# The end of the last output product: token tile by token tile, with four stores of 256 KB

## The reference

```
def rms_norm_2(x, g):
    xf = x.astype(jnp.float32)
    y = xf * lax.rsqrt(jnp.mean(xf * xf, axis=-1, keepdims=True) + RMS_EPS)
    return (y * g.astype(jnp.float32)).astype(x.dtype)

def swiglu_ffn(x, w_in, w_out):
    gate, up = jnp.split(x @ w_in, 2, axis=-1)
    return (jax.nn.silu(gate) * up) @ w_out

# second_block, for each of two layers; h after the last one is the result, 256 x 1024
        normed = rms_norm_2(h, ffn_norm_pre[layer])
        h = h + rms_norm_2(swiglu_ffn(normed, ffn_w_in[layer], ffn_w_out[layer]), ffn_norm_post[layer])
```

## Time and profile before

| | us |
|---|---|
| median of 3 runs | 1220.99 (1220.68 to 1221.53) |
| the profiled execution | 1221.12 |
| its span | 1219.1 |
| PE busy in the span | 1185.5 (97%) |
| DVE, ACT, POOL busy | 758.5, 600.0, 151.6 |

### The profile page before, as it was taken

One profiled execution on the slowest core, in us unless ns is written; L12 is line 12 of the kernel. 1 busy time (PEld: TensorE's weight loads), 2 busy tenths in 40 slices (PEclk: granted clock), 3 DMA queues, 4 the chain that ended last, 5 costly groups with the idle time before them and its releaser, 6 DMA issues.

```text
span 1219.1 us, 19296 instructions
## 1 busy us (share of the span) xinstructions
PE 1185.5 (97%) x7504; PEld 1052.2 (86%) x7504; DVE 758.5 (62%) x1049; ACT 600.0 (49%) x862; POOL 151.6 (12%) x175
## 2 busy tenths in 40 slices
PE   6999999998999999999999999999799989999997
PEld 6999999997888887888888888888799968888885
DVE  5667544376887555564535777764676866777752
ACT  6665553434544444543434544443566756445431
POOL 2000000051123001211100111100101101111100
PEclk9999999999999999999999999999899999999999
DMA  9455344543555654645435455465444234554540
GB/s 355 176 208 190 105 139 173 176 168 139 178 202 177 245 184 160 227 160 186 173 133 212 156 176 195 180 220 194 146 153 160 70 109 173 211 198 172 179 166 34
DMA packets 31975, 212.06 MB, mean 174 GB/s; under 512 B 4169, under 2 KB 4829, under 8 KB 7592
## 3 DMA queue, kind: packets, MB, share of 16 engines
q1 hardware_dynamic: 28936, 201.68, 46.6%
q0 software_dynamic: 2688, 9.26, 2.2%
q10 hardware_dynamic: 288, 0.23, 0.1%
HBM read 210.08 MB, written 1.08 MB: 173 GB/s over the span
## 4 chain that ended last, share of the span: by engine, by line
PE 86%; issue 6%; DVE 3%; ACT 2%; POOL 2%; DMA 1%; SPq 0%; DVEq 0%; POOLq 0%; ACTq 0%
PE acc L446 41%; PE acc L585 17%; PE acc L587 8%; PE aux L446 8%; PE acc L486 1%; POOL gate L795 1%; PE acc L488 1%; PE acc L490 1%; PE acc L539 1%; PE acc L536 1%; PE acc L541 1%; PE aux L2579 1%; PE aux L2640 1%; PE aux L2228 1%; ACT wh L419 1%
## 5 line engine op out<-in xcount | busy, mean ns | idle before, releaser
L427 DVE TENSOR_TENSOR wl<-raw,wh 128x2048 fp32r<-128x2048 f32 x129 | 295.2, 2294 | 259.7 <-ACT wh L419 253.0
L419 ACT ACTIVATE wh<-raw 128x2048 fp32r<-128x2048 f32 x190 | 362.7, 1912 | 144.9 <-PE acc L446 109.9
L585 PE MATMUL acc<-hx,wh 128*128 128x512 f32 x864 | 305.4, 399 | 0.0
L587 PE MATMUL acc<-hx,wl 128*128 128x256 f32 x864 | 242.7, 281 | 0.0
L446 PE MATMUL acc<-hx,wh 128*128 128x256 f32 x1280 | 234.6, 285 | 1.9 <-DVE hx L662 1.9
L446 PEld LDWEIGHTS acc<-hx,wh 128*128 128x128 f32 x1280 | 200.7, 193 | 3.4 <-DVE wl L427 2.1
L585 PEld LDWEIGHTS acc<-hx,wh 128*128 128x128 f32 x864 | 162.4, 188 | 40.4
L446 PE MATMUL acc<-hx,wl 128*128 128x256 f32 x640 | 181.7, 284 | 0.0
L587 PEld LDWEIGHTS acc<-hx,wl 128*128 128x128 f32 x864 | 163.2, 189 | 0.0
L434 DVE TENSOR_TENSOR wl<-raw,wh 128x1024 fp32r<-128x1024 f32 x122 | 151.9, 1245 | 1.5 <-ACT wh L419 1.0
L446 PEld LDWEIGHTS acc<-hx,wl 128*128 128x128 f32 x640 | 123.3, 193 | 0.0
(11 more groups left out here) (382 smaller groups left out, 1948.2 us busy)
## 6 DMA issues: line engine op xcount, KB each, us to landing
raw<-in_stream SPq DMA_DIRECT2D x190, 1024.0 KB, 4.8
bias_b<-in_bias POOLq DMA_DIRECT2D x6, 512.0 KB, 4.6
grow<-in_grows POOLq DMA_DIRECT2D x4, 512.0 KB, 4.3
nbias<-strip POOLq DMA_DIRECT2D x4, 512.0 KB, 4.6
x<-in_x SPq DMA_DIRECT2D x2, 512.0 KB, 4.0
y<-x SPq DMA_DIRECT2D x1, 1024.0 KB, 3.9
s<-cums POOLq DMA_DIRECT2D x1, 512.0 KB, 4.2
decay<-in_decay POOLq DMA_DIRECT2D x1, 512.0 KB, 3.8
```

Source lines behind the costliest of these rows:

```text
L419: nc.scalar.activation(wh[:, s, :], raw[:, s, :], ACT.Copy).then_inc(hi_ready, 1)
L427: nc.vector.tensor_tensor(wl[:, s, :], raw[:, s, :], wh[:, s, :].bitcast(F32), ALU.subtract).then_inc(lo_ready, 1)
L585: nc.tensor.matmul(out[:, :], wh[:, s, cols], hx[:, k].rearrange("p a n -> p (a n)"), start=(k == 0), stop=False, skip_group_check=True)
L587: last = nc.tensor.matmul(out[:, 0:SEQ], wl[:, s, cols], hh[:, k, :], start=False, stop=(k == KT - 1), skip_group_check=True)
```

## The change

PE runs the last two chunks of the last layer's output product token tile by token tile: tile 0 of o0+9 and of o0+10, then tile 1 of both. The other layer's product keeps its order. The last norm uses the form by token tile on ACT, DVE and POOL. SP issues four stores of 128 rows by 512 columns (256 KB), in the order tile 0 left, tile 0 right, tile 1 left, tile 1 right, each behind the semaphore of the instruction that writes that part of `x`, and waits for all four.

```diff
-            sp.wait_ge(post_done, 4 * TT)
-            sp.dma_start(io["out"].rearrange("(t p) d -> p t d", p=P), x[:]).then_inc(y_out, 16)
-            sp.wait_ge(y_out, 16)
+            for t in range(TT):
+                for half in range(2):
+                    cols = slice(half * WW, (half + 1) * WW)
+                    sp.wait_ge(*((post_done, 3 * TT + t + 1) if half else (x_half, 2 * TT + t + 1)))
+                    sp.dma_start(io["out"][t * P:(t + 1) * P, cols], x[:, t, cols]).then_inc(y_out, 16)
+            sp.wait_ge(y_out, 16 * 2 * TT)
@@ pool
-            post(3)
+            for t in range(TT):
+                pool.wait_ge(mean_in, 2 * TT + t + 1)
+                g.tensor_tensor(rstd[:, t:t + 1], psum1[:, t:t + 1], mhalf[:, 0:1], ALU.pow).then_inc(mean_pow, 1)
@@ scalar
-            post(3, "ffn_out_1", (6, 5), fjunk, 1)
+            o0 = START["ffn_out_1"]
+            for c in range(o0 + 4, o0 + 9):
+                split_hi(act, c)
+            for t in range(TT):
+                tile_square(3, "ffn_out_1", 0, t, fjunk)
+            for c in range(o0 + 9, o0 + 11):
+                split_hi(act, c)
+            for t in range(TT):
+                tile_square(3, "ffn_out_1", 1, t, fjunk)
@@ vector
-            post(3, "ffn_out_1", (6, 5), mixed2, grow2, 1)
+            o0 = START["ffn_out_1"]
+            dve.wait_ge(grow_in[4], 16)
+            for c in range(o0 + 4, o0 + 9):
+                split_lo(dve, c)
+            for t in range(TT):
+                tile_mix(3, "ffn_out_1", 0, t, mixed2, grow2)
+            for c in range(o0 + 9, o0 + 11):
+                split_lo(dve, c)
+            for t in range(TT):
+                tile_mix(3, "ffn_out_1", 1, t, mixed2, grow2)
+                tile_x(2, 3, "ffn_out_1", t, mixed2)
@@ tensor
-                for i in range(5):
-                    product_w(pe, o0 + 6 + i, g0 + 2, hid2h, hid2l, 2 + WKT * i, WKT, FFN_KT, second=True)
+                def second_half(i, toks=(0, 1)):
+                    product_w(pe, o0 + 6 + i, g0 + 2, hid2h, hid2l, 2 + WKT * i, WKT, FFN_KT, toks=toks, second=True)
+
+                for i in range(3):
+                    second_half(i)
+                for toks in ((0,), (1,)) if layer else ((0, 1),):
+                    for i in (3, 4):
+                        second_half(i, toks)
```

## The result

| | before | changed |
|---|---|---|
| median, 13 runs each | 1220.74 (1218.46 to 1222.01) | 1218.28 (1215.31 to 1218.93) |
| ratio | | 0.9978, 95% interval 0.997 to 0.9987 |
| span of the profiled execution | 1219.1 | 1216.2 |
| end of the last matmul | 1210.43 | 1210.70 |
| tail: from there to the end of the span | 8.67 | 5.53 |

What follows compares the result with a forecast made beforehand. PE, busy 97% of the span, bounds the kernel, so the change works in the 8.67 us behind the last matmul. Gains 0.22 + 1.06 + 1.7 = 2.98, call it 3.0, take 1220.99 to 1218.0; range 1217.2 to 1219.3.

Steps and rivals of the forecast that it cites:

- PE's order: Last two chunks on PE: running them tile by tile costs 0 and was booked as gaining 0.
- the margin of 0.4: On DVE in the old PE order: tile 0's `x` done at 1210.8, before DVE is wanted for tile 1 at 1211.18.
- Sum and power: Last norm, tile 1: from sum to `x` takes 0.88 instead of 1.10, a gain of 0.22.
- `x` by halves: DVE behind the last power: two instructions of 512 columns, 1.42, instead of two of 1024, 2.48; gain 1.06.
- The landing: Last store, issue to semaphore: 256 KB land in 2.2 instead of the large store's 3.9; gain 1.7.
- my 0.2 on top: Last store's landing: 0.2 added to 1.98 for rows of 2 KB and any lateness of the third store.
- the first rival: Last store: landing mostly fixed, about 3.0 or 3.2, total gain 2.2, time 1218.8; chance 0.12.
- A mostly fixed landing: Last store: 256 KB land in about 3.0 or 3.2, total gain 2.2, time 1218.8; chance 0.12.
- stores in a row: SP's queue: each store begins only when the one ahead has landed; time 1225.3 at landings of 3.9; chance 0.03.
- a cost at PE's turns: Last product on PE: one matmul's spacing, 0.23, at each of three turns, 0.7 in all; no chance of its own.
- the 2.6 that the prediction worked out: Last store's landing by the Trainium skill's formula, about 2.0 fixed plus bytes at 436 GB/s; total gain then 2.6.

Runs made afterwards that it cites:

- e1: The changed kernel with PE's old order, both token tiles of the right half ending in the last chunk: median 1218.71, ratio to before 0.9979, tail 5.54.
- e3: The kernel before with only its store changed, to one 512 KB store for each token tile: median 1218.96, ratio to before 0.9984, tail 7.39.
- e8: The changed kernel with tile 1 written and stored in quarters, issued by SP and ACT, and its square's wait for tile 0's removed: 1217.11, ratio 0.9972, tail 5.44.
- e2: The changed kernel with all of `x` stored in one 1 MB DMA once both tiles are written: median 1219.41, ratio to before 0.9991, tail 7.50.
- e4: The changed kernel with two stores of 512 KB, one for each token tile, instead of four: median 1218.61, ratio to before 0.9976, tail 6.17.
- e5: The changed kernel with its four 256 KB stores all issued behind the last write of `x`: median 1219.96, ratio to before 0.9994, tail 7.51.
- e9: The changed kernel run once more, unaltered: median 1217.96, ratio to before 0.998, tail 5.53.
- e7: The changed kernel with tile 1's last 512 columns written in two instructions and stored in two 128 KB stores: median 1217.33, ratio to before 0.9968, tail 5.55.

## Why the prediction was right

The steps behind the last matmul were the right ones but for one wait that was left out, the largest miss of a term was 0.2, and the measured 1218.28 lies near the forecast 1218.0.

**PE's order, cost 0.** Right: 0.0 idle in the last product, and the same 54.66 us between its fixed points as before. That tile 0's earlier end brings nothing either, and the margin of 0.4 without it, e1 shows with 0.41.

**Sum and power, 0.22.** Right: 0.88 from sum to `x`, as read where `nsa_out` ends.

**`x` by halves, 1.06.** Right: 1.41, last issue 0.03 later. Tile 0's part stood where it was put, 0.34 later than written (1205.36 for 1205.02), 0.27 of it PE's and 0.06 the wait's, next.

**A term that was missing.** The square starts 0.10 behind the end of PE and not 0.04, so the first part of the tail is 0.06 longer. In the chain of waits of the changed kernel a wait of its own stands ahead of tile 0's square:

```profile
1205.30 0.02 ACTq L611
1205.31 0.04 issue
1205.36 0.70 ACT fjunk L1216 x2
```

The new form puts two waits ahead of tile 1's square, where the old one had only the one for PE. The old form shows 0.04 (e3: 1209.34 to 1209.38), every kernel with the new form 0.10, and e8, which takes the second wait away, 0.04. I had called the new wait harmless because what it waits for is long over. An extra wait cost 0.06 on ACT even then, and SP's in e2, e4 and e5 cost 0.05.

**The landing, 2.2.** Mis-sized by my 0.2 on top: it was 2.0, the lower end of 1.98. Rows of 2 KB cost 0.02 to 0.04 of it. The lesson of e4 and e3 is the same: a start, the bytes at the rate, an end. The split of the large store read off the windows (0.89 and 0.45) is a little off: its first packet starts 0.92 behind the issue and its last one ends 0.35 ahead of the semaphore, with 2.64 between them, and the sum is the same 3.9. POOL's rows of 3.0 and 3.2, which held the first rival up, said nothing of this queue.

**The sum.** The tail was forecast at 8.67 - 2.98 = 5.69 and came to 5.53. The landing was 0.2 shorter than put, the wait cost 0.06, and 0.02 is the rounding of the last 0.41: 5.69 - 0.21 + 0.06 - 0.02 = 5.52, 0.01 short of the measured. That the span agrees so well (1216.2 for 1216.1) is luck: PE's last matmul ended 0.27 later, where the prediction had wanted it within 0.1 of 1210.43, and that hid the tail's 0.16. The same kernel's other profiled execution (e9) has a span of 1215.7.

**The rivals.** A mostly fixed landing is refuted by 3.9, 2.6, 2.0 and 1.7 for four sizes; stores in a row by e5 (a last landing 3.9 behind the first issue, where a row would need 8.0); a cost at PE's turns by the missing idle time. The rule of the Trainium skill ("DMA: Bandwidth & Descriptors", section on measured bandwidth) to batch to 1 MiB or more has a measured price here: 0.02 us for four stores instead of one when both start at once (e5 against e2), against 1.97 gained by starting three of them early. The page gives its fixed cost of about 2.0 for DMAs that GpSimd issues; SP issued these, and by their landings it is 1.3 to 1.4. So the 2.6 that the prediction worked out with it was a figure for another way of issuing.

**What moves the end of PE's work.** It moves by up to 2 us between kernels whose PE work is the same, long before the last product. The windows show two of the steps (granted TensorE clock third from the end), first before, then changed:

```profile
280.00:300.00 20.00, 17.66 (x85) 14.51 (x86) 11.68 (x14) 8.98 (x17) 0.87 (x2) 1.00 0.49 188
985.00:1001.00 16.00, 12.21 (x70) 9.44 (x71) 7.81 (x21) 9.25 (x16) 0.00 (x0) 0.89 0.09 39
...
280.00:300.00 20.00, 17.66 (x73) 14.17 (x74) 10.25 (x9) 7.36 (x10) 0.87 (x2) 0.91 0.49 185
985.00:1001.00 16.00, 11.80 (x83) 9.50 (x83) 9.20 (x25) 9.04 (x16) 0.00 (x0) 1.00 0.19 71
```

By POOL's timelines the changed kernel is 0.06 ahead at 253.7, 1.58 behind at 301.5, 1.91 behind at 948.7 and 0.28 behind at 1018.6. So it loses 1.6 where its granted clock is below 1.00 (2.4 GHz for a part of the stretch, 1.2 for the rest), and gains 1.6 back where that of the kernel before did. e3, e4, e7, e8 and e9 have the first of these stretches too, at 0.91, and lose about 1.6 there; e1, e2 and e5 have neither and lose nothing. As e1 and e5 differ from the changed kernel in the last 17 us alone, the stretch isn't of the change's making. Most of the rest, -1.2 to +2.1 against the kernel before, is there by 93 us, and 0.1 to 0.4 comes between 884 and 907; what makes these, and why the clock falls in one execution and not in another, stays open.

## What to carry to other kernels

Behind the last matmul everything is serial, so each microsecond there counts in full; list its steps, and for each ask what share of it belongs to the last piece of data alone. Cut work and stores so that all but the last piece lies beside the matmuls, and stop cutting where the steps run at one pace: here writing `x` (0.26 MB in 0.71 us, 370 GB/s) and storing it (382 GB/s) do, and the two finer cuts tried gained nothing (e7) and about 0.02 (e8 without its shorter wait). When a gain of 0.25% is to be judged, compare the stretch that the change touches, since ends of the same upstream work differ by as much as the gain.

## What the runs showed of the hardware

- A store's landing from SP is 3.9, 2.6, 2.0 and 1.7 us for 1024, 512, 256 and 128 KB. From the issue to the first packet it is 0.84 (256 KB) to 0.92 (1 MB), and 0.35 from the end of the last packet to the semaphore. Stores in flight share one stream of bytes without a gap (e5).
- SP's issues with nothing between them stand 0.38 to 0.50 apart (e5), and 0.45 held a fifth store up (e7).
- A second wait, for a semaphore that had been reached before, delayed what stands behind it by 0.06 on ACT (0.10, against 0.04 in e8) and by 0.05 on SP (e2, e4, e5).
- DVE takes 1.41 for 512 columns twice in this form, 1.54 with one of them cut in two (e7) and 1.67 with both (e8): each extra cut of `x` costs 0.13.
